# Gate and up products by one level of Strassen's scheme in a streaming encoder step, on one Trainium2 core

## The reference, cut to what matters

```python
def _swiglu(h, w_gate, w_up, w_down):
    return (jax.nn.silu(h @ w_gate) * (h @ w_up)) @ w_down
...
y_p = y_p + _merge(fox_o, gla_o, gr, gla_norm_g[layer], w_out[layer])
y_p = y_p + _swiglu(_rmsnorm(y_p, norm2_g[layer]), w_gate[layer], w_up[layer], w_down[layer])
...
y_prompt = _rmsnorm(y_p, final_norm_g)
```

## Time and profile before

| | us |
|---|---|
| time, median of 3 runs (range) | 3362.28 (3362.01 to 3363.81) |
| the profiled execution's own time | 3358.64 |
| its span | 3356.9 |
| its mean granted TensorE clock | 0.959 |
| PE busy, DVE busy, ACT busy, POOL busy | 3084.2, 2053.2, 1188.7, 508.0 |

### The profile page before, as it was taken

One profiled execution on the slowest core, in us unless ns is written; L12 is line 12 of the kernel. 1 busy time (PEld: TensorE's weight loads), 2 busy tenths in 40 slices (PEclk: granted clock), 3 DMA queues, 4 the chain that ended last, 5 costly groups with the idle time before them and its releaser, 6 DMA issues. The chain is left out here.

```text
span 3356.9 us, 49447 instructions
## 1 busy us (share of the span) xinstructions
PE 3084.2 (92%) x18905; PEld 2852.9 (85%) x18905; DVE 2053.2 (61%) x3540; ACT 1188.7 (35%) x2361; POOL 508.0 (15%) x404
## 2 busy tenths in 40 slices
PE   7999999959999956889978999999998999999996
PEld 5899999947777734677768999999998999999995
DVE  5232212759999833677744666666666666666665
ACT  6353111238888712444432222222224322222223
POOL 0010000000000001321202222222222322222223
PEclk9999999969999977899998999999999999999998
DMA  4235422253242082344435111111133311111112
GB/s 123 73 135 185 148 58 58 51 114 83 63 96 63 1 266 66 111 140 141 144 100 176 51 44 44 50 44 46 48 127 115 107 50 44 44 50 44 44 37 77
DMA packets 280252, 290.37 MB, mean 86 GB/s; under 512 B 32473, under 2 KB 246806, under 8 KB 271040
## 3 DMA queue, kind: packets, MB, share of 16 engines
q1 hardware_dynamic: 277464, 281.12, 28.8%
q10 hardware_dynamic: 1344, 4.36, 0.6%
q0 software_dynamic: 1296, 2.88, 0.3%
HBM read 200.40 MB, written 87.92 MB: 86 GB/s over the span
## 5 line engine op out<-in xcount | busy, mean ns | idle before, releaser
L2376 PE MATMUL ps_ffn<-h,wsp_n 128*128 128x312 f32 (+1 forms) x6336 | 1048.7, 321 | 23.9 <-DMA h<-h2T 23.0
L2376 PEld LDWEIGHTS ps_ffn<-h,wsp_n 128*128 128x128 f32 x6336 | 1011.4, 189 | 27.4 <-issue 23.4
L2302 DVE TENSOR_TENSOR yacc<-ps_ffn,yacc 128x312 f32<-128x312 f32 (+1 forms) x1008 | 489.5, 519 | 386.2 <-PE ps_ffn L2394 386.1
L660 PE MATMUL ps_project<-hT,wsp 128*128 128x416 f32 (+1 forms) x3000 | 602.1, 357 | 0.0
L660 PEld LDWEIGHTS ps_project<-hT,wsp 128*128 128x128 f32 (+1 forms) x3000 | 548.2, 186 | 23.5 <-issue 7.8
L2394 PE MATMUL ps_ffn<-aT,dsp 128*128 128x312 f32 (+1 forms) x3168 | 550.1, 323 | 4.0 <-DVE yacc L2302 3.1
L2394 PEld LDWEIGHTS ps_ffn<-aT,dsp 128*128 128x128 f32 x3168 | 509.5, 189 | 8.0 <-DVE yacc L2302 3.7
L2278 ACT ACTIVATE aT<-a 128x416 fp32r<-128x416 f32 x132 | 65.1, 494 | 821.1 <-DVE a L2353 821.1
L2181 POOL TENSOR_TENSOR wsp_n<-wraw_n,wsp_n 128x1024 fp32r<-128x1024 f32 x88 | 211.8, 2408 | 815.7 <-ACT wsp_n L2222 815.7
L2344 DVE RECIPROCAL silu<-silu 128x416 f32<-128x416 f32 x132 | 304.9, 2310 | 30.1 <-ACT silu L2267 30.0
L1001 ACT ACTIVATE pexp<-ps_fox,ntop 128x512 f32<-128x512 f32 (+2 forms) x320 | 198.6, 621 | 52.9 <-DVE ntop L1044 51.1
(11 more groups left out here) (258 smaller groups left out, 3447.3 us busy)
## 6 DMA issues: line engine op xcount, KB each, us to landing
wraw_n<-in_w_gate_dram SPq DMA_DIRECT2D x44, 512.0 KB, 3.9
wraw_n<-in_w_up_dram SPq DMA_DIRECT2D x44, 512.0 KB, 3.8
draw<-in_w_down_dram SPq DMA_DIRECT2D x44, 512.0 KB, 3.4
h2T<-hT_m SPq DMA_DIRECT2D x16, 1024.0 KB, 5.3
zT<-zs SPq DMA_DIRECT2D x12, 1040.0 KB, 4.1
wraw<-in_w_in_dram SPq DMA_DIRECT2D x24, 512.0 KB, 4.5
h<-h2T SPq DMA_DIRECT2D x8, 1248.0 KB, 12.6
qk_hi<-work SPq DMA_DIRECT2D x8, 1024.0 KB
```

The costliest lines, as they stand in the source:

```text
L660: last = pe.matmul(ps[0:w, p % NB, 0:BLK], wsp[:, b, s, k, 0:w], hT[:, g * TPB:(g + 1) * TPB, v, k, :], start=k == 0 and m == 0, stop=k == ...
L2302: dve.tensor_tensor(y, z, y, ALU.add).then_inc(added, 1)
L2376: last = pe.matmul(ps[:, 2 * q + s, 0:FB[b] * TT], wsp[:, par, s, w, k, :], h2[:, v, k, cols(b)], start=m == 0, stop=m == 3 * KD - 1)
```

## The change

`ffn` runs over four groups of 520 tokens, each cut into two halves of 260 columns. The features are taken in 11 pairs of 128 + 128, so one pair and one of the two weight matrices (a "cell") is a product of 2 x 2 blocks: weights A (two feature blocks by two halves of the model width) times inputs B (two halves of the width by two halves of the tokens). It is computed with seven block products in place of eight. There are 4 x 11 x 2 = 88 cells, gate and up in turn. For each cell DVE forms four sums of weight blocks (`sum_w`, 128 x 512 each), ACT copies seven high parts and POOL subtracts seven low parts (`low_w`, 128 x 512), PE runs seven products of 12 matmuls, and DVE makes the four results from them (`combine`, seven instructions, into `cs` in SBUF; ACT takes the first product out of its bank). The input operands `hop` (seven, of 128 x 1040) are made once a group, in the last cell of the group before, with four sums and seven splits.

The seven products use six PSUM banks in turn. A down product is an item of 6 matmuls (two feature blocks by three passes, in one bank) of 260 columns; items alternate between the two other banks, and an item waits until the one two before it was added (`item_out`). `silu`, `make_a` and `low_a` read and write SBUF. The rows at a group's end are items too, the final gain moves from POOL to DVE (`gain`), and the loops are unrolled. In `gla_merge` ACT writes `h2T` unsplit and `low_h` is gone.

```diff
-            def low_h(c, e):
-                L = width(c)
-                dve.wait_ge(h_high, 2 * c + e + 1)
-                dve.tensor_tensor(hT[:, LO, 4 * e:4 * e + 4, 0:L], ps[:, B_O, :].rearrange("p (k t) -> p k t", k=4)[:, :, 0:L],
-                                  hT[:, HI, 4 * e:4 * e + 4, 0:L].bitcast(F32), ALU.subtract).then_inc(h_low, 1)
...
@@ ffn, DVE @@
+            def sum_w(c, j):
...
+                if j == 0:
+                    dve.wait_ge(w_come[b][A21], v)
+                    dve.wait_ge(w_come[b][A22], v)
+                    dve.tensor_tensor(wsum[:, 0], wraw[:, b, A21], wraw[:, b, A22], ALU.add).then_inc(w_sum, 1)
...
+            def low_h(q, i):
+                dve.wait_ge(h_hi, NPROD * q + i + 1)
+                dve.tensor_tensor(hop[:, i, LO], h_block(i), hop[:, i, HI].bitcast(F32), ALU.subtract).then_inc(h_low_v, 1)
...
+            def combine(c, what):
...
+                out, partial, i = {
+                    U2: (u2[:], p1[:], P6),
+                    V2: (v2[:], u2[:], P5),
+                    C11: (cs[:, s, 0, 0:FH], p1[:], P2),
+                    U3: (u3[:], u2[:], P7),
+                    C22: (cs[:, s, 1, FH:FT], v2[:], P7),
+                    C21: (cs[:, s, 1, 0:FH], u3[:], P4),
+                    C12: (cs[:, s, 0, FH:FT], v2[:], P3)}[what]
+                dve.tensor_tensor(out, product_bank(c, i), partial, ALU.add).then_inc(combined, 1)
+            def silu(u, j):
...
+                dve.reciprocal(sg[:, j], sg[:, j]).then_inc(inv_done, 1)
+                dve.wait_ge(inv_done, n)
+                dve.tensor_tensor(sg[:, j], cs[:, 0, f, t * FH:(t + 1) * FH], sg[:, j], ALU.mult).then_inc(silu_done, 1)
+            def make_a(u, j):
...
+                dve.tensor_tensor(x, x, sg[:, j], ALU.mult).then_inc(a_made, 1)
+            def add(n, first, dd, t):
+                y, z = yacc[:, dd, t * FH:(t + 1) * FH], ps[:, 6 + n % 2, 0:FH]
+                dve.wait_ge(item_done, n + 1)
...
+                    dve.tensor_tensor(y, z, y, ALU.add).then_inc(item_out, 1)
+            def gain(n, t, half):
+                y = row_buffer(t)[:, half]
...
+                dve.scalar_tensor_tensor(out=y, in0=y, scalar=inv[:, t:t + 1], in1=grow[:, half * 512:(half + 1) * 512],
+                                         op0=ALU.mult, op1=ALU.mult).then_inc(y_done, 1)
@@ ffn, POOL @@
+            def low_w(c, i):
+                raw = wsum[:, S_OF[i]] if i in S_OF else wraw[:, c % 2, A_OF[i]]
+                pool.wait_ge(w_hi, NPROD * c + i + 1)
+                pool.tensor_tensor(wop[:, i, LO], raw, wop[:, i, HI].bitcast(F32), ALU.subtract).then_inc(w_lo, 1)
...
+            for c in range(NCELL + 1):
...
+                for i in range(NPROD):
+                    if c + 1 < NCELL:
+                        low_w(c + 1, i)
+                    if i == 1 and c:
+                        low_d(c - 1)
+                    if turn and i in (O_B21, O_T3, O_B22):
+                        low_h(q, i)
@@ ffn, PE @@
+            def cell_product(c, i):
...
+                for k in range(KH):
+                    for m, (w, v) in enumerate(PASSES):
+                        last = pe.matmul(product_bank(c, i), wop[:, i, w, k, :], hop[:, i, v, k, :],
+                                         start=k == 0 and m == 0, stop=k == KH - 1 and m == 2)
+                last.then_inc(product, 1)
+            def down(n, u, dd, t):
+                h, c = divmod(dd, 4)
+                pe.wait_ge(a_lo, 4 * u + (J12 if t else J21) + 1)
+                pe.wait_ge(d_lo, 2 * u + h + 1)
+                if n >= 2:
+                    pe.wait_ge(item_out, n - 1)
...
+            for c in range(NCELL):
+                cell_product(c, P1)
+                item(c, 0)
+                cell_product(c, P5)
+                item(c, 1)
+                cell_product(c, P6)
+                cell_product(c, P2)
+                item(c, 2)
+                item(c, 3)
+                cell_product(c, P7)
+                item(c, 4)
+                item(c, 5)
+                cell_product(c, P4)
+                item(c, 6)
+                cell_product(c, P3)
+                item(c, 7)
```

More of the change, by code:

```diff
@@ L1977, in _ @@
                     gate(t)
[L1983 to L2010, removed]
-    return next(k for k, ts in enumerate(BATCHES[half]) if t in ts)
+NG4 = 4
@@ new lines, in row_cell, with items_before, down_item, row_item @@
+def row_cell(c):
+    return c >= 2 * NPAIR and (c - 1) % (2 * NPAIR) < 2 and 2 * NPAIR < c < NCELL
+def items_before(c):
+    return ITEMS * (c - 2) + NROW * sum(row_cell(i) for i in range(c))
+def down_item(c, k):
+    return items_before(c) + k + (sum(r < k for r in ROW_AFTER) if row_cell(c) else 0)
+def row_item(c, i):
+    return items_before(c) + ROW_AFTER[i] + 1 + i
+def row_quarter(c):
+    return (c - 1) // (2 * NPAIR) - 1
+def late_down(t, k):
+    return items_before(NCELL) + (k if t == 0 else ITEMS + k + k // 2)
@@ L2170, in _ @@
+            for t in range(NROW):
+                store(NG4 - 1, t)
+            for t in range(NROW):
+                sp.wait_ge(y_stored[t], 16 * (NG4 + (t == NROW - 1)))
         @block.gpsimd
@@ new lines, in _ @@
+            low_a(NU - 1, J12)
+            for k in range(ITEMS):
+                add(late_down(0, k), False, k, 0)
+            for k in range(ITEMS):
+                add(late_down(1, k), False, k, 1)
+                if k % 2:
+                    t, half = divmod(k // 2, 2)
+                    row(late_row(t, half), NG4 - 1, t, half)
+            n = NG4 - 1
+            sum_squares(LATE[0], n, 2 * NROW * n + 4)
+            row(late_row(2, 0), n, 2, 0)
+            row(late_row(2, 1), n, 2, 1)
@@ new lines, in down @@
+            def down(n, u, dd, t):
[4 more added lines that the diff above has]
+                    pe.wait_ge(item_out, n - 1)
+                for f in range(2):
+                    for m, (w, x) in enumerate(PASSES):
+                        last = pe.matmul(ps[:, 6 + n % 2, 0:FH], dsp[:, h, w, f, c * P:(c + 1) * P], aT[:, u % 2, x, f, t * FH:(t + 1) * FH],
+                                         start=f == 0 and m == 0, stop=f == 1 and m == 2)
+                last.then_inc(item_done, 1)
@@ new lines, in row, with item @@
+            def row(n, t, half, ready):
+                pe.wait_ge(item_out, max(ready, n - 1))
+                for c in range(4):
+                    last = pe.transpose(ps[0:TT, 6 + n % 2, c * P:(c + 1) * P], yacc[:, 4 * half + c, t * TT:(t + 1) * TT], ident[:])
+                last.then_inc(item_done, 1)
+            def item(c, k):
+                if c >= 2:
+                    t, dd = divmod(k, 4)
+                    down(down_item(c, k), c // 2 - 1, 4 * (c % 2) + dd, t)
+                    if row_cell(c) and k in ROW_AFTER:
+                        i = ROW_AFTER.index(k)
+                        row(row_item(c, i), i, (c - 1) % (2 * NPAIR), items_before(c))
```

816 lines of the change are left out of this document (473 added, 343 removed).

## The result

| | before | after |
|---|---|---|
| median, range | 3362.61 (3362.01 to 3363.81), 4 runs | 3455.48 (3454.17 to 3460.19), 4 runs |
| span of the profiled execution | 3356.9 | 3452.5 |
| first instruction of `ffn` | 1761.4 | 1748.1 |
| step of 24 matmuls, or pair of cells | 34.24 | 35.14 |

The changed kernel is slower by 92.9 us, a ratio of 1.0278 (95% interval 1.026 to 1.0296). Forecast were 3607 us and a range of 3420 to 3750: direction and range held, but the forecast change of +245 us was 2.6 times the measured one.

What follows compares the result with a forecast made beforehand. PE set the old pace; DVE blocked by POOL would set the new one. Pairs +205, changes of group +67, start +9, tail -19, `gla_merge` -17 gave +245 us on the median: 3607 us, range 3470 to 3730 (3420 to 3750 leaving out 2 in 10).

Steps and rivals of the forecast that it cites:

- start: Beginning of `ffn`, loading and splitting first weights and inputs: second cell ends at about 50 us against 40.6 before, +9 us.
- 43 pairs: Regular gate and up cell pairs of `ffn`: each 39.0 us in place of a 34.24 us step, +205 us.
- changes of group: Three switches between token groups in `ffn`: 32 us each, 96 against 29 before, +67 us.
- T: Time of a regular pair of cells in `ffn`: 39.0 us, with a range of 37 to 41.5.
- PE's 32.0 us a pair: PE in a pair of `ffn` cells: 264 matmuls of 260 columns at 0.121 us, 32.0 us if nothing waits.
- DVE's own work of 27.0 us: DVE in a pair without blocking: item adds, combines, `sum_w`, reciprocals and 12 others, together 27.0 us.
- the two exclude each other: DVE instructions with two SBUF operands and POOL subtractions in `ffn` block each other; 20 such DVE instructions a pair.
- My equation: Pair time T from DVE's 27.0 us plus 20 waits of 0.74 us, weighted by 22.2 / (T - 10): 38.4 us.
- the 0.6 us for the clock: Addition to each pair for PE's lower granted clock after pauses, 0.6 us, taking T to 39.0.
- mild rival: POOL's work falls behind DVE's reciprocals and bank reads, halving waits: T = 35.5, near 3440 us; 13%.
- My walk through the order: Written order of both cells: gate about 18.2 us, up about 20.5, with item 4 waiting some 4 us.
- worse rival: Blocking and PE's pauses feed each other: T = 44, changes of group at +100, near 3870 us; 9%.

Runs made afterwards that it cites:

- experiment 1: Changed kernel with POOL's `low_w` and `low_d` cut to 16 columns from the second cell on; 3324.52 us.
- experiment 7: Changed kernel with both of POOL's `low_d` of a pair moved from behind the second to behind the fifth weight block of each cell; 3639.31 us.
- experiment 8: Changed kernel with only the up cell's `low_d` moved to the cell's end, the gate cell's left in place; 3635.01 us.
- experiment 4: Changed kernel with the input sums, high and low parts at the three changes of group cut to 8 columns of each row; 3415.18 us.

## Why the prediction was right and wrong

The difference of the spans, 95.6 us, splits as follows. The start ends here where the third cell would have begun without a wait, 4.3 us before its 24-matmul group.

| term | forecast | measured | from |
|---|---|---|---|
| 43 pairs | +205 | +39 | 43 x (35.14 - 34.24) |
| changes of group | +67 | +70 | 99 - 29 |
| start | +9 | +20 | 1808.8 - 1748.1, less 40.6 |
| tail | -19 | -18 | 36.2 - 53.9 |
| last cell, without the waits of a regular one | | -2 | |
| `gla_merge` | -17 | -13 | 1748.1 - 1761.4 |
| sum | +245 | +96 | |

**The term that was mis-sized is T: 39.0 forecast, 35.14 measured.** It alone puts the sum 166 us too high; the other terms take 17 of that back, 11 of them by a wait at the start that I had missed. The step that failed is the share of DVE's instructions that meet POOL. The parts of T:

- PE's 32.0 us a pair was right: a cell without waits takes 15.9.
- DVE's own work of 27.0 us was right. With the blocked 5.6 it makes 32.6, and DVE was busy 195.9 / 6 = 32.6 us a pair.
- That the two exclude each other was right, and shown by experiment 1. The length of a blocking too: eight of the 20 instructions of a pair were blocked, 0.7 us each, where I had 0.74. (My equation gives 38.5 with these terms, not 38.4.)
- How often they meet was wrong. I had let POOL's work fall evenly over the time, so that 22.2 / 28.4 = 78% of DVE's instructions, 15.6 of 20, would meet it. Eight did, the same eight in each of 29 regular pairs. 5.6 us in place of 11.5 are more than the error of T: DVE also waited, some 2.5 us a pair, which my sum did not have, and the 0.6 us for the clock did not come in this kernel. POOL isn't independent of DVE: of its 65 idle us in the six pairs (211.0 less 145.75), 57.2 stand ahead of a summed block, waiting for ACT, which waits for DVE's `sum_w`:

```profile
L2194 POOL TENSOR_TENSOR wop<-wsum,wop 128x512 fp32r<-128x512 f32 x48 | 66.3, 1381 | 57.2 <-ACT wop L2232 57.2
```

  So POOL's idle time falls where DVE has just been, or is, at these instructions. Counted in the trace: POOL is idle 31% of the six pairs, but 66 of the 120 instructions with two SBUF operands begin in that time, 11 of the 12 free ones of each pair. Of the other 54, which begin while POOL runs, 48 were blocked. The mild rival had half of my waits and 3440 us. It was the right one in size, with 35.5 for T, but not by the mechanism that I named for it: reciprocals and bank reads fill 53% of the six pairs, and 56% of POOL's work falls beside them, hardly more than chance would give.
- My sum also took blocked time for the price, since DVE had to pay all of it. It isn't the price. In the table above 5.6 us blocked go with 3.1 us above PE's 32.0, 8.3 with 2.1, 7.6 with 7.7, and 4.1 with 7.7. Priced is what is late where PE waits, which are the add of item 2 and the low part of J21 here. A long wait costs once more, through the clock (experiments 7 and 8, the two with 7.7). My walk through the order had named the first of them, at some 4 us in place of 1.45, and not the second.

The Trainium skill's rule (SBUF — State Buffer, "Who interferes with whom") held in every run: with two SBUF operands DVE was blocked where POOL was at a subtraction, and the combines and item adds, which read a bank, kept 0.41 to 0.43 us throughout.

**What would show it.** DVE in the chain and busy near 90%: yes, 47% of the chain there against PE's 39%, and 93% busy. Means of `sum_w`, `make_a`, `low_a` over the free ones, combines and adds unchanged, `low_w` over 1.29 (1.42 and 1.48): yes. PE waits for `yacc` in up cells: yes, and for `aT`. Starts 39 us apart: no. Clock below 1.00 there: no, it was 1.00 in the regular stretch, as waits of 1.4 us didn't lower it; 0.89 in the 35 us in which a change of group begins. The second price that I had put at 0.6 us was nothing behind these waits of 1.4 us, and 2.4 us behind one of 3.87 (experiment 7).

**Sums beside T.** My own range of 3470 to 3730 is not what its terms give: T from 37 to 41.5 with all other terms at their bounds is 3456 to 3799. The worse rival's numbers give 3855, not 3870. None of this touches the failed term.

**Changes of group.** The sum of 32 each was right (33), but not its split. I had some 15 for the inputs and 17 for rows and gains. Measured were 17.4 for the long cell and 15 behind it, and 5.0 of the 17.4 stay without the work, most of them beside three blocked instructions (experiment 4).

**Start.** I had followed the first two cells: the second ended 46.5 us after the first instruction of `ffn` (50 forecast). The third cell's first item needs the low part of the first pair's J21:

```profile
1782.55 12.02 PE L2591 MATMUL ps_ffn<-hop,wop 128*128 128x260 f32 x96 [2.85 <-issue]
...
1808.18 1.67 PE L2603 MATMUL ps_ffn<-aT,dsp 128*128 128x260 f32 x6 [10.05 <-DVE aT L2405]
```

PE runs the first two cells without items, ahead of DVE, and then waits 10.05 us. That wait is missing from my sum. Cutting POOL's work short (experiment 1) left 55.6 us of the 60.7; since that run leaves the first cell's work whole, it shows only that blocking from the second cell on is at most some 5 us of it.

## What to carry to other kernels

When two engines exclude each other, don't multiply shares of busy time: in a fixed periodic order most instructions meet the other engine always or never (here the same 8 of 20 in each pair), so write both orders down against the clock, also with who releases whom. Then price only what stands ahead of an instruction for which the bounding engine waits, and add the slower clock behind a long wait (seen behind 2.89 us before the change and behind 3.87 here, not behind 1.4); the same blocked microseconds cost little elsewhere. A scheme that saves matmuls pays if the added sums and splits leave the second engine slack: here taking the reciprocals off DVE and moving two instructions turned 1.0278 into 0.9948, and a further order gave 0.9924.

## What the runs showed of the hardware that was not expected

- Moving two POOL subtractions of 2.4 us by three products changed the whole by 184 us (3455 to 3639), with the same work on every engine. Half of the difference a pair is PE's longer waits, half the granted clock of 0.50 behind them.
- Three instructions of DVE with 32 elements a partition took 1.28, 1.29 and 2.27 us beside POOL and 0.19 away from it.
- With less work of its own DVE was blocked longer: 5.6 us a pair with the reciprocals, 8.3 without.
- After a wait of 3.87 us 12 matmuls of 260 columns took 2.80 us, at a granted clock of 0.50; after one of 1.4 us the following product took its usual 1.61.
